# The layer norm of the conformer block: first mean copied between the diagonals, last tiles on VectorE, sums placed between the squares, row sums turned one by one

## The reference

```
a = h @ w_pw1 + b_pw1
g = a[..., :D_MODEL] * sigmoid(a[..., D_MODEL:])
y = depthwise_conv(g, w_dw, width 31) + b_dw
mu  = mean(y, axis=-1)                     # over the 1024 channels of a token
var = mean(square(y - mu), axis=-1)
y = silu((y - mu) * rsqrt(var + EPS) * ln_g + ln_b)
op = y @ w_pw2 + b_pw2
```

## Time and profile before

| | us |
|---|---|
| median of 3 runs (lowest, highest) | 1654.76 (1654.35, 1655.68) |
| the profiled execution | 1652.92 |
| its span | 1651.1 |
| PE busy | 1611.0 (98%) |
| DVE busy | 930.2 (56%) |
| ACT busy | 667.9 (40%) |
| POOL busy | 287.4 (17%) |

### The profile page before, as it was taken

The page is one execution under the profiler, slowest core; times in us unless marked ns, Lnnn a source line. Parts: engine busy times, 40 slices in busy tenths (PEclk is TensorE's granted clock), DMA queues, the critical chain, the costliest instruction groups (busy, mean ns, idle before and its releaser), DMA issues.

```text
span 1651.1 us, 26203 instructions
## 1 busy us (share of the span) xinstructions
PE 1611.0 (98%) x11087; PEld 1559.3 (94%) x11087; DVE 930.2 (56%) x1580; ACT 667.9 (40%) x1002; POOL 287.4 (17%) x343
## 2 busy tenths in 40 slices
PE   8989999999999999999999999989999999999998
PEld 6988889899999999999999999969999999999998
DVE  5556767766776644554358989967742232223232
ACT  3436545553544423432246656755432211221122
POOL 0001111000165524452342122230000000000000
PEclk9999999999999999999999999989999999999999
DMA  9322233132254434433333289873222222221211
GB/s 318 97 69 77 86 98 103 35 115 77 91 165 140 149 120 135 143 126 122 122 122 90 72 181 183 172 150 69 78 77 77 77 77 77 77 77 60 88 59 64
DMA packets 140141, 178.12 MB, mean 108 GB/s; under 512 B 12753, under 2 KB 116889, under 8 KB 139000
## 3 DMA queue, kind: packets, MB, share of 16 engines
q1 hardware_dynamic: 117824, 109.68, 20.9%
q0 software_dynamic: 21872, 66.66, 16.2%
q10 hardware_dynamic: 328, 0.10, 0.0%
...
## 4 chain that ended last, share of the span: by engine, by line
PE 82%; DVE 10%; DMA 3%; ACT 3%; issue 1%; POOL 0%; SPq 0%; DVEq 0%; ACTq 0%; POOLq 0%
PE PS L687 25%; PE PS L689 24%; PE PS L692 24%; DVE YACC L2295 5%; DMA ZACC<-ZTAP 2%; PE PS L757 1%; PE PS L1010 1%; PE PS L784 1%; PE PS L1021 1%; DMA Y<-SHIFT 1%; DMA XROWS<-in_x_sample 1%; PE PS L973 1%; DVE GP L2259 0%; PE PS L846 0%; DVE HL L1883 0%
## 5 line engine op out<-in xcount | busy, mean ns | idle before, releaser
L687 PE MATMUL PS<-HH,WH 128*128 128x320 f32 x1776 | 410.7, 313 | 4.8 <-DVE HL L1883 4.4
L689 PE MATMUL PS<-HL,WH 128*128 128x320 f32 x1776 | 405.1, 309 | 0.0
L692 PE MATMUL PS<-HH,WL 128*128 128x320 f32 x1776 | 403.8, 309 | 0.0
L1735 DVE TENSOR_TENSOR WL<-RAW,WH 128x2048 fp32r<-128x2048 f32 (+2 forms) x87 | 196.1, 2254 | 204.8 <-ACT WH L1271 204.7
L687 PEld LDWEIGHTS PS<-HH,WH 128*128 128x128 f32 x1776 | 296.1, 189 | 8.1 <-issue 5.7
L689 PEld LDWEIGHTS PS<-HL,WH 128*128 128x128 f32 x1776 | 298.4, 188 | 0.0
L692 PEld LDWEIGHTS PS<-HH,WL 128*128 128x128 f32 x1776 | 298.2, 189 | 0.0
L1271 ACT ACTIVATE WH<-RAW 128x2048 fp32r<-128x2048 f32 (+2 forms) x95 | 171.6, 1806 | 112.7 <-PE PS L692 112.7
L1899 DVE SCALAR_TENSOR_TENSOR X<-PS,MODV,X 128x128 f32<-128x128 f32 (+2 forms) x192 | 72.4, 434 | 198.7 <-PE PS L692 198.6
L609 POOL TENSOR_TENSOR BGACC<-BGACC,BGW 128x512 f32<-128x512 f32 x98 | 135.0, 1377 | 197.0 <-ACT BGW L1526 195.9
L687 PE MATMUL PS<-HIDH,WH 128*128 128x320 f32 x704 | 162.2, 311 | 0.7 <-DVE HIDL L2218 0.7
(11 more groups left out here) (320 smaller groups left out, 2292.4 us busy)
## 6 DMA issues: line engine op xcount, KB each, us to landing
...
```

The costliest lines, as they stand in the source:

```text
L687: mm(o, wh, xh, start=first, stop=False)
L689: mm(o, wh, xl, start=False, stop=False)
L692: ins = mm(o, wl, xh, start=False, stop=last)
L1735: V.tensor_tensor(WL[:, u % 2, 0:n], RAW[:, u % 2, 0:n], WH[:, u % 2, 0:n].bitcast(F32), ALU.subtract).then_inc(lo_done, 1)
```

## The change

1. The PSUM tile `shift` is copied by ACT after diagonal 11 of tile 7 (`SHIFT_DIAGS = 12`) instead of after diagonal 17, and only once: `SHIFT7` is gone, and PE multiplies `SHIFT` with a matrix of sevens (`SEVENS`, set by DVE) instead.
2. ACT's `negated` for the last of the low parts (unit 9, pw2 tiles 2 and 3) moves from ahead of these diagonals to behind the third square, and POOL's transfer for it (`unit_low`) from ahead of the `OFFSET` transfers to behind them.
3. DVE adds `SHIFT` onto tile 6 too (between `SUM += Y` and its taps of tile 7) and squares tile 7; POOL shifts six tiles, ACT squares seven. `SUM` ends at tile 6: DVE's addition of tile 7 is gone, and PE adds tile 7 from `Y` with matmuls of its own.
4. PE's sums of the tiles come between the second and the third pair of squares, into a PSUM tile of their own for the rows (`srow`), and the mean is finished by two 128x320 matmuls with tile 7 behind the transposes.
5. The rows are copied and turned in two pieces, sums first, then squares. DVE computes the squared mean from the first piece while the second is copied. It needs two fewer instructions between the second piece and the inverse root.
6. The table load for SiLU moves from ahead of the squares to behind the copy of `OFFSET`.

The diff, cut to its core:

```diff
+SHIFT_DIAGS = 12
...
-    o += [("stat", "ln"), "mu", ("turn", "ln"), ("rb", "ln")] + [("pw2", m) for m in range(KT)] + ffn(1)
+    o += ["mu", ("srow", "ln"), ("stat", "ln"), ("turn", "ln"), ("rb", "ln")] + [("pw2", m) for m in range(KT)] + ffn(1)
...
@block.gpsimd
-            pool.wait_ge(sem("shift_made"), 1)
-            for i in range(KT - 1):
-                if i >= SUM_BY_DMA:
-                    was_read(pool, ("cv", i))
-                    pool.wait_ge(sem("sq_added"), NORMS["mu"] - 1)
+            was_read(pool, "shift")
+            for i in range(SUM_BY_DMA):
                 pool.dma_start(Y[:, i, :], SHIFT[:], accum_op=ALU.add).then_inc(y_shifted[i], 16)
-            unit_low(KT - 1 + LOW_BY_DMA)
             was_read(pool, "mu")
             for i in range(CENTRE_BY_DMA, KT):
-                pool.wait_ge(sem("sq_made"), SQ_BASE["ln"] + i + 1)
+                if i < KT - 1:
+                    pool.wait_ge(sem("sq_made"), SQ_BASE["ln"] + i + 1)
+                else:
+                    pool.wait_ge(sem("last_squared"), 1)
                 pool.dma_start(Y[:, i, :], OFFSET[:], accum_op=ALU.add).then_inc(y_centred[i], 16)
+            unit_low(KT - 1 + LOW_BY_DMA)
...
@block.tensor
+            def mean_part(w, x, first, last):
+                for i in range(2):
+                    ins = mm(mean[:, i, 0:HALF], w[:], x[:, i * HALF:(i + 1) * HALF], start=first, stop=last)
+                return ins
...
-            for k in range(0, KT - 2, 2):
-                square_sums(k)
-            for i in range(2):
-                mm(mean[:, i, 0:HALF], ONES[:], SHIFT7[:, i * HALF:(i + 1) * HALF], start=True, stop=False)
+            square_sums(0)
+            square_sums(2)
+            pe.wait_ge(sem("sevens_set"), 1)
+            mean_part(SEVENS, SHIFT, True, False)
             pe.wait_ge(sem("sq_added"), NORMS["mu"])
+            mean_part(ONES, SUM, False, False).then_inc(mm_done, 1)
             for g in range(GROUPS):
-                mm(rows[COLG * g:COLG * (g + 1), 1, 0:3 * P], ONES[:, 0:COLG], (SUM, SHIFT7)[g // 2][:, halves3[g % 2]],
-                   start=True, stop=True)
+                mm(means[COLG * g:COLG * (g + 1), 0, 0:3 * P], (ONES, SEVENS)[g // 2][:, 0:COLG], (SUM, SHIFT)[g // 2][:, halves3[g % 2]],
+                   start=True, stop=g >= 2)
+            square_sums(4)
+            pe.wait_ge(sem("last_shifted"), 1)
+            for g in range(2):
+                ins = mm(means[COLG * g:COLG * (g + 1), 0, 0:3 * P], ONES[:, 0:COLG], Y[:, KT - 1, halves3[g]], start=False, stop=True)
+            ins.then_inc(mm_done, 1)
             square_sums(KT - 2).then_inc(mm_done, 1)
...
-            was_read(pe, ("stat", "ln"))
-            for b in range(2):
+            for b, n in ((1, ("srow", "ln")), (0, ("stat", "ln"))):
+                was_read(pe, n)
                 for i in range(3):
                     ins = tr(ps[:, b, i * P:(i + 1) * P], LNROW[:, b, i * P:(i + 1) * P], EYE[:])
-            ins.then_inc(mm_done, 1)
+                ins.then_inc(sem("means_turned") if b else mm_done, 1)
+            mean_part(ONES, Y[:, KT - 1, :], False, True).then_inc(sem("mean_whole"), 1)
             hold_clock(rows, HOLD)
...
@block.scalar
                 if i == KT - 1:
                     tap_diagonals(i, 0, FIRST_DIAGS)
+                    round_units(U[("glu", i)] + 2)
+                    tap_diagonals(i, FIRST_DIAGS, SHIFT_DIAGS)
+                    filled(act, "shift")
+                    A(row2(SHIFT[:]), tile2("shift")[:, :, 0:HALF], ACT.Copy, scale=-1.0 / (SUM_BY_DMA * P)).then_inc(free_of("shift"), 1)
+                    tap_diagonals(i, SHIFT_DIAGS)
+                    continue
...
+            for i in range(KT - 1):
+                act.wait_ge(y_shifted[i], 16)
                 A(LNQ[i][:], Y[:, i, :], ACT.Square).then_inc(sem("sq_made"), 1)
-            n = ("stat", "ln")
-            filled(act, n)
-            A(LNROW[:], tile2(n)[:, :, 0:3 * P], ACT.Copy).then_inc(free_of(n), 1)
-            filled(act, "mu")
+                if i == 2:
+                    negated(KT - 1 + LOW_BY_DMA)
+            for b, n in ((1, ("srow", "ln")), (0, ("stat", "ln"))):
+                filled(act, n)
+                A(LNROW[:, b, :], tile2(n)[:, 0, 0:3 * P], ACT.Copy).then_inc(free_of(n), 1)
+            act.wait_ge(sem("mean_whole"), 1)
             A(row2(OFFSET[:]), tile2("mu")[:, :, 0:HALF], ACT.Copy, scale=-1.0 / D).then_inc(free_of("mu"), 1)
+            A(LNSS[:, 0:1], ONES[:, 0:1], ACT.Silu)
...
@block.vector
                     V.tensor_tensor(SUM[:], SUM[:], Y[:, i, :], ALU.add).then_inc(sem("sq_added"), 1)
+                    V.memset(SEVENS[:], KT - 1.0).then_inc(sem("sevens_set"), 1)
+                    was_read(dve, "shift")
+                    V.tensor_tensor(Y[:, i, :], Y[:, i, :], SHIFT[:], ALU.add).then_inc(y_shifted[i], 16)
...
-            add_sum(KT - 1, None, Y[:, KT - 1, :])
+            V.tensor_tensor(LNQ[KT - 1][:], Y[:, KT - 1, :], Y[:, KT - 1, :], ALU.mult).then_inc(sem("last_squared"), 1)
...
+            dve.wait_ge(sem("means_turned"), 1)
+            link(token_sums(1))
+            link(V.scalar_tensor_tensor(out=RS[:, 2, 0:6], in0=HST[:, 6:12], scalar=1.0 / (D * D), in1=HST[:, 6:12],
+                                        op0=ALU.mult, op1=ALU.mult))
+            link(V.tensor_scalar(RS[:, 3, 0:6], RS[:, 2, 0:6], 1.0, -EPS, ALU.mult, ALU.add))
             filled(dve, n)
...
+            token_sums(0).then_inc(free_of(n), 1)
```

More of the change, by code:

```diff
@@ L327, in program @@
         LNQ = [sb(f"LNQ{i}", [P, TOK], R_HL + i * TOK * 4) for i in range(KT)]
-        SHIFT, SHIFT7, OFFSET = [sb(n, [P, TOK], R_HH + i * TOK * 4) for i, n in enumerate(("SHIFT", "SHIFT7", "OFFSET"))]
+        SHIFT, OFFSET = [sb(n, [P, TOK], R_HH + i * TOK * 4) for i, n in enumerate(("SHIFT", "OFFSET"))]
+        SEVENS = sb("SEVENS", [P, P], R_HH + 2 * TOK * 4)
         LNROW = sb("LNROW", [P, 2, 3 * P], R_T[0])
@@ L487, in program @@
         NORMS, DIAGS, nsum, ndiag = {}, {}, 0, 0
-        for n, adds in (("ck", KVT), ("cq", QLT), ("ffn0", KT), ("mix1", KT), ("mu", KT - SUM_BY_DMA + 1), ("ffn1", KT)):
+        for n, adds in (("ck", KVT), ("cq", QLT), ("ffn0", KT), ("mix1", KT), ("mu", KT - SUM_BY_DMA), ("ffn1", KT)):
             nsum += adds - 1
@@ L494, in program @@
         SQ_BASE, nsq = {}, 0
-        for n, tiles in (("mix0", KT), ("ck", KVT), ("cq", QLT), ("ffn0", KT), ("mix1", KT), ("ln", KT), ("ffn1", KT)):
+        for n, tiles in (("mix0", KT), ("ck", KVT), ("cq", QLT), ("ffn0", KT), ("mix1", KT), ("ln", KT - 1), ("ffn1", KT)):
             SQ_BASE[n] = nsq
@@ L1214, in _ @@
             halves3 = (slice(0, 3 * P), slice(2 * P, TOK))
-            rows, mean = begin(("stat", "ln")), begin("mu")
+            mean, means, rows = begin("mu"), begin(("srow", "ln")), begin(("stat", "ln"))
             def square_sums(k):
-                pe.wait_ge(sem("sq_made"), SQ_BASE["ln"] + k + 2)
+                if k < KT - 2:
+                    pe.wait_ge(sem("sq_made"), SQ_BASE["ln"] + k + 2)
+                else:
+                    pe.wait_ge(sem("sq_made"), SQ_BASE["ln"] + KT - 1)
+                    pe.wait_ge(sem("last_squared"), 1)
                 for g in range(GROUPS):
@@ L1674, in _ @@
                 if i:
-                    tap_diagonals(i, FIRST_DIAGS if i == KT - 1 else 0)
-                    if i - 1 < SUM_BY_DMA:
-                        conv_out(i - 1)
-            filled(act, "shift")
-            for dst, tiles in ((SHIFT, 1.0), (SHIFT7, KT - 1.0)):
-                ins = A(row2(dst[:]), tile2("shift")[:, :, 0:HALF], ACT.Copy, scale=-tiles / (SUM_BY_DMA * P))
-                if dst is SHIFT:
-                    ins.then_inc(sem("shift_made"), 1)
-            ins.then_inc(free_of("shift"), 1)
-            A(HST[:, 0:1], ONES[:, 0:1], ACT.Silu)
-            for i in range(KT):
-                if i < KT - 1:
-                    act.wait_ge(y_shifted[i], 16)
-                else:
-                    act.wait_ge(sem("last_shifted"), 1)
-                A(LNQ[i][:], Y[:, i, :], ACT.Square).then_inc(sem("sq_made"), 1)
-            n = ("stat", "ln")
-            filled(act, n)
-            A(LNROW[:], tile2(n)[:, :, 0:3 * P], ACT.Copy).then_inc(free_of(n), 1)
-            filled(act, "mu")
+                    tap_diagonals(i)
+                    conv_out(i - 1)
+            for i in range(KT - 1):
+                act.wait_ge(y_shifted[i], 16)
+                A(LNQ[i][:], Y[:, i, :], ACT.Square).then_inc(sem("sq_made"), 1)
+                if i == 2:
[4 more added lines that the diff above has]
+            act.wait_ge(sem("mean_whole"), 1)
             A(row2(OFFSET[:]), tile2("mu")[:, :, 0:HALF], ACT.Copy, scale=-1.0 / D).then_inc(free_of("mu"), 1)
+            A(LNSS[:, 0:1], ONES[:, 0:1], ACT.Silu)
             spread_copy(("rb", "ln"), RSTD, QT)
```

22 lines of the change are left out of this document (9 added, 13 removed).

## The result

| | median us | lowest to highest | runs |
|---|---|---|---|
| before | 1654.55 | 1652.76 to 1655.68 | 4 |
| changed | 1645.62 | 1644.67 to 1646.86 | 4 |

The ratio is 0.9947, with a 95% interval of 0.9932 to 0.9963: 8.9 us faster. Forecast were 1647.0, with a range of 1645.4 to 1650.5. The profiled execution of the changed kernel took 1646.86, with a span of 1645.0.

What follows compares the result with a forecast made beforehand. PE's path from convolution to pw2 waited on SHIFT transfers. Gains of 7.1 us to the end of the squares and 0.7 from turning rows make 7.8: 1654.76 - 7.8 = 1647.0; own range 1645.7 to 1648.5, 8-in-10 range 1645.4 to 1650.5.

Steps and rivals of the forecast that it cites:

- pair 2: PE's second pair of squares: waits for tile 3's square at 1092.5 us, ends at 1093.25.
- mean parts: PE's two matmuls for the mean behind the second pair of squares: 1.25 us each, to 1095.75.
- rows of sums: PE's matmuls putting the tiles' sums into rows, ahead of the third pair of squares: 0.76 us, to 1096.5.
- end of pair 4: PE finishes the last pair of squares at 1098.8 us instead of 1105.90, a gain of 7.1.
- spread: PE's step ahead of RSTD's copy, scale and SiLU: starts at 1103.9 us instead of 1111.74, behind hold_clock.
- Part 1: ACT's copy of shift moves earlier, so POOL's SHIFT additions start 5.4 us earlier and land each 1.78.
- rival C: SHIFT transfers behind the last ZACC transfer land late or slowly: up to 7.7 us lost, 1654.7; chance 6%.
- Part 2: Squares on ACT and DVE: all there by 1095.95 us; DVE's shift of tile 6 costs nothing, at most 1.2.
- Part 3: PE's order from first to fourth pair of squares: PE itself the bound from 1092.5 us, gain 7.1.
- rival B: PE's clock stays low: mild form 2 us, 1649.0, chance 7%; until the spread 12.3 us, 1659.3, chance 2%.
- Part 4: Rows copied and turned in two pieces between the last squares and the spread: saves 0.7 us.
- Rival A: Late last low part stalls PE ahead of pw2 tile 2; each us past 1123.7 costs one; chance 10%.

Runs made afterwards that it cites:

- e7: Kernel before with only the copies of shift moved up to diagonal 12, negated moving with them: stretch 21.66 us against 26.33, median 1647.72, ratio 0.9962.
- e1: Changed kernel with the copy of shift back behind the last of the eighteen diagonals: stretch 23.09 us against 17.99, median 1650.13, ratio 0.9972.
- e11: Changed kernel run again without edits, its ZACC transfer late: stretch 18.58 us against 17.99, median 1645.76, ratio 0.9941.
- e8: Changed kernel with the square of tile 7 on ACT again, behind tile 6's: stretch 18.03 us against 17.99, 1645.33 in one run.
- e2: Changed kernel with PE's sums of the tiles behind the third pair of squares: stretch 21.79 us against 17.99, median 1648.86, ratio 0.9958.
- e9: Changed kernel with both of ACT's row copies waiting for the last squares: stretch 18.43 us against 17.99, 1645.47 in one run.
- e3: Changed kernel with POOL's last low part held until ACT's SiLU of tile 7: 538.1 us from pw2 to the end against 533.7, median 1649.05, ratio 0.9965.

## Why the prediction was right

By its own steps, counted from the end of the convolution:

| step starts at | predicted | measured |
|---|---|---|
| pair 2 | 1.44 | 1.74 |
| mean parts | 2.19 | 2.52 |
| rows of sums | 4.69 | 4.87 |
| pair 3 | 5.44 | 5.54 |
| tile 7's rows | 6.19 | 6.18 |
| end of pair 4 | 7.74 | 7.64 |
| spread | 12.84 | 12.41 |
| pw2 | 18.54 | 17.99 |

- **Part 1, the early copy**, was right in mechanism: copy, first square 4.9 later, one tile each 1.8. Pair 2 came 0.3 later than forecast: the copy stood 9.99 and not 10.26 ahead of the convolution's end, and the first square 4.92 and not 4.7 behind it. The 4.7 came from before, where POOL's queue was empty; with the early copy it is the `ZACC` transfer that sets it, which the text named only to argue against rival C. Alone the early copy is worth 4.67 in the kernel before (e7), and 5.10 in the changed one (e1; 4.51 against e11).
- **Part 2, the squares**, cost nothing, as said; e8 shows it for tile 7's. The memset took 0.17. The transfers had 1.2 to spare ahead of pair 3 (tile 5's square ends at 1097.5, PE takes it at 1098.78) where 1.4 was forecast; in e11 it was some 1.3.
- **Part 3, PE's order**, was right, and its terms ran a little high: 0.67 for the rows of sums where 0.76 was taken, 2.35 for both mean parts where 2.5 was, and 1.46 for tile 7 with pair 4 where 1.5 was. The like rows of tile 7 and of pair 4 start 0.02 apart (1099.42 and 1099.44), so the narrow matmuls of the two run side by side.
- **The clock** stayed at 1.00, as expected against rival B. But the text gave it no share of the gain. Against e11, e7 has 1.6 of 3.08 by it, and e2 1.7 of 3.80. The forecast contained it without naming it, because the steps were priced from rows at the full level.
- **Part 4, turning the rows**: 4.77 from the end of pair 4 to the spread, where 5.1 was forecast and 5.84 stood before. As forecast, PE's own `hold_clock` ended last and not DVE. The 0.3 are the transposes, with the last mean part starting 1.01 behind pair 4 where 1.15 was taken, and that mean part at 1.08 where 1.25 was taken. e9 gives 0.38 for the early piece alone. That DVE needs fewer instructions was not tried by itself.
- **Behind the spread** 5.58 against 5.65. The table load (1103.89 + 1.28) and its small instruction ended 1.6 ahead of the copy of `RSTD`: hidden, with 1.8 to spare in the forecast.
- **Rival A** stood 2.4 away, where 2.3 was forecast. Its mechanism is real (e3) and its price steeper than forecast: 4.4 for a wait of 2.6.
- **The term left out**: moving `negated` also freed the diagonal behind `first_mean`, 0.3 in the convolution of tile 7, which the prediction took to run as before (0.92 a tap from 1079.9).
- **The sum**: 8.34 in the stretch where 7.8 was forecast, 8.9 by the medians. The mis-sized terms, all small, are part 4 (0.3) and the groups of part 3 (0.4 together), less the 0.3 lost at pair 2; they and the 0.1 behind the spread make the 0.55 that is over. The 0.3 ahead of the stretch comes on top, and the last 0.3 of the 8.9 lies within the spread of the runs.

The mechanism was right, but how near the number came is in part luck. The prediction's own narrow range, 1645.7 to 1648.5, just misses the 1645.62, and the wide one holds it by 0.2. Its small errors partly cancelled. At the late level of e11 the stretch of the same kernel is 7.75 shorter than before, so the forecast's 7.8 lies within what two profiles of one kernel differ by.
